# A mixture-of-experts stage in one block, with unscaled rows stored early and two weight places filled before the routing

## What is computed

```python
h = rmsnorm(x, ffn_norm)                              # x * rsqrt(mean(x^2) + eps) * ffn_norm
g_logits = hf @ wg_router + bg_router                 # 4 groups
g_sel = argmax(g_logits); g_w = softmax(g_logits)[g_sel]
e_in = (hf @ we_router + be_router)[:, g_sel]         # 8 experts of that group
top_v, top_i = top_k(e_in, 2)
top_w = softmax(top_v) * g_w
for each of the 32 experts:                           # 1024 -> 256 -> 1024
    hid = silu(hf @ w_gate) * (hf @ w_up) * gates     # gates: top_w of the two chosen experts, else 0
    out += hid @ w_down
x = x + out
```

## Time and profile before

| | us |
|---|---|
| time, median of 3 runs (lowest, highest) | 1571.29 (1565.78, 1571.32) |
| the profiled execution's own time | 1570.89 |
| its span, first to last instruction | 1569.1 |
| PE busy in the span (share) | 1443.5 (92%) |
| DVE busy (share) | 747.6 (48%) |
| ACT busy (share) | 408.3 (26%) |
| POOL busy (share) | 50.4 (3%) |
| bytes moved by DMA | 206.15 MB, mean 131 GB/s |
| granted clock of PE, mean | 0.976 |

### The profile page before, as it was taken

The page is one execution under the profiler, slowest core; times in us unless marked ns, Lnnn a source line. Parts: engine busy times, 40 slices in busy tenths (PEclk is TensorE's granted clock), DMA queues, the critical chain, the costliest instruction groups (busy, mean ns, idle before and its releaser), DMA issues. The chain is left out here.

```text
span 1569.1 us, 13363 instructions
## 1 busy us (share of the span) xinstructions
PE 1443.5 (92%) x4754; PEld 688.1 (44%) x4754; DVE 747.6 (48%) x1657; ACT 408.3 (26%) x645; POOL 50.4 (3%) x120
## 2 busy tenths in 40 slices
PE   7999999999999999999999999998999775998782
PEld 3455555555555544544444344445444433333220
DVE  5567677777676734210134349965333422221113
ACT  2444435444444250000010133133302330000000
POOL 0000000000000000000000000000000001222111
PEclk9999999999999999999999999999999987999996
DMA  7122111221201142222142122010125247999995
GB/s 277 41 97 64 41 49 46 94 65 57 59 22 41 40 175 80 67 70 78 67 160 81 34 80 67 14 58 31 41 73 211 88 195 282 420 427 428 430 410 194
DMA packets 38098, 206.15 MB, mean 131 GB/s; under 512 B 7312, under 2 KB 8336, under 8 KB 30608
## 3 DMA queue, kind: packets, MB, share of 16 engines
q1 hardware_dynamic: 31840, 192.68, 32.8%
q0 software_dynamic: 5040, 8.40, 1.4%
q10 hardware_dynamic: 1152, 4.19, 0.7%
HBM read 202.63 MB, written 12.58 MB: 137 GB/s over the span
## 5 line engine op out<-in xcount | busy, mean ns | idle before, releaser
L442 PE MATMUL gla_proj<-hT,weight_slots 128*128 128x512 f32 x864 | 378.1, 592 | 1.9 <-DVE hT L805 1.9
L442 PEld LDWEIGHTS gla_proj<-hT,weight_slots 128*128 128x128 f32 x864 | 160.9, 190 | 188.8 <-issue 188.1
L907 PE MATMUL bl_p<-hT,weight_slots 128*128 128x512 f32 x256 | 114.3, 600 | 2.1 <-PEq L166 2.1
L2437 PE MATMUL ex_p_gu<-weight_slots,ex_rowsT 128*64 128x512 f32 x432 | 98.6, 604 | 16.7 <-DMA weight_slots<-in_w_gu 14.2
L1268 PE MATMUL mid_p_proj<-hT,weight_slots 128*128 128x512 f32 x208 | 94.7, 604 | 2.3 <-DVE hT L1436 2.3
L907 PEld LDWEIGHTS bl_p<-hT,weight_slots 128*128 128x128 f32 x256 | 48.8, 192 | 62.8 <-issue 62.8
L2573 DVE TENSOR_TENSOR ex_hidden<-ex_silu,ex_p_gu 128x256 f32<-128x256 f32 x16 | 6.7, 421 | 133.9 <-ACT ex_silu L2530 133.9
L596 ACT ACTIVATE gla_level_decay<-gla_level_decay 128x1024 f32<-128x1024 f32 x56 | 59.0, 1057 | 39.3 <-DVE gla_level_decay L725 38.9
L2437 PEld LDWEIGHTS ex_p_gu<-weight_slots,ex_rowsT 128*64 128x64 f32 x432 | 31.6, 138 | 74.9 <-issue 60.0
L1268 PEld LDWEIGHTS mid_p_proj<-hT,weight_slots 128*128 128x128 f32 x208 | 39.7, 193 | 53.8 <-issue 52.7
L943 ACT ACTIVATE bl_sig<-bl_p 128x512 f32<-128x512 f32 x16 | 9.6, 597 | 196.0 <-PE bl_p L907 196.0
(11 more groups left out here) (404 smaller groups left out, 1939.5 us busy)
## 6 DMA issues: line engine op xcount, KB each, us to landing
weight_slots<-in_w_gu SPq DMA_DIRECT2D x27, 2048.0 KB, 29.7
weight_slots<-in_w_dn SPq DMA_DIRECT2D x12, 2048.0 KB, 32.7
weight_slots<-in_w_gla SPq DMA_DIRECT2D x40, 512.0 KB, 3.6
weight_slots<-in_w_merge SPq DMA_DIRECT2D x32, 512.0 KB, 3.9
weight_slots<-in_w_out SPq DMA_DIRECT2D x16, 512.0 KB, 4.5
weight_slots<-in_w_v SPq DMA_DIRECT2D x3, 2048.0 KB, 7.4
xT<-in_w_dn SPq DMA_DIRECT2D x3, 2048.0 KB, 49.3
hT<-in_w_gu SPq DMA_DIRECT2D x3, 2048.0 KB, 19.8
```

The costliest lines, as they stand in the source:

```text
L442: last = nc.tensor.matmul(pj[:, n % 2, :], lhsT, rhs, start=(k == 0), stop=(k == KT - 1))
L907: last = nc.tensor.matmul(pp[:, m % 4, :], core.slot(slot)[:, k, :], src[:, k, :], start=(k == 0), stop=(k == KT - 1))
L2437: last = nc.tensor.matmul(pG[rows, e, :], hgT[:, k, rows], core.as_gate_up(at[k // 4])[:, x, k % 4, :], start=(k == 0), stop=(k == KT - 1))
```

## The change

The three blocks become one. `routing_programs`, `expert_programs` and `combine_programs` return one function for each engine, and `moe_stage` calls them one after the other on each engine, with no barrier between:

```diff
+def moe_stage(core, omT, x_rows, gate, most, ix, ixg, hg, hg_in, out):
+        lot = Lot(core, ctx)
...
+        with nc.Block() as block:
             @block.sync
             def _(sp):
...
+                route[0](sp)
+                experts[0](sp)
+                load_and_store(sp)
```

**SP.** Parts 8 and 9 are issued behind the small loads, ahead of part 4; a place of a first half is free when that half is used; the combination starts when the scatters have landed:

```diff
-                sp.dma_start(iota[:], dram["moe_iota"][:]).then_inc(aux, 16)
+        sp.dma_start(iota, dram["moe_iota"][:, 0:CAP]).then_inc(aux, 16)
+        for c in (8, 9):
+            core.load_part(sp, c)
...
-                sp.wait_ge(h_stored, 16 * NB)
-                core.load_part(sp, 8)
...
-                    core.load_part(sp, PLACES - 1)
...
-                        sp.wait_ge(gu_done if kind == "g" else d_done, u + 1)
+                sp.wait_ge(d_done if kind == "d" else gu_done if h else gu_half, u + 1)
...
+                if k == KT // 2 - 1:
+                    last.then_inc(gu_half, 1)
...
+        first_round()
+        sp.wait_ge(lot.most_ready, 1)
+        with sp.If(sp.value_load(most[0:1, 0:1], min_val=0, max_val=T) > CAP):
...
+        for e in range(2):
+            sp.wait_ge(y_out[e], first_out)
```

**ACT.** The rows are stored as they are turned, without 1 / rms, in three pieces of 512, 256 and 256 columns, and the scaled copies go:

```diff
+        def store(lo, hi):
+            act.dma_start(h_rows[:, :, lo:hi], x_rows[:, :, lo:hi]).then_inc(h_stored, 16)
...
+            if i == 3:
+                store(0, 512)
+            if i == 5:
+                store(512, 768)
+            if i == KT - 1:
+                store(768, D)
...
-                for n in range(NB):
-                    nc.scalar.activation(h_rows[:, n], x_rows[:, n], ACT.Copy, scale=rs[:, n:n + 1]).then_inc(h_scaled, 1)
-                    act.wait_ge(h_scaled, n + 1)
-                    act.dma_start(core.h_rows[n * P:(n + 1) * P, :], h_rows[:, n]).then_inc(h_stored, 16)
```

**1 / rms for the experts.** A second list carries it to the slots: DVE multiplies the one-hot table of the units with `rs`, PE sums it by slot, and each pair's column is copied to `rs2` ahead of the turned rows. It scales gate inside `silu` and up inside `hidden`:

```diff
+        nc.vector.tensor_tensor(four, four, rs.unsqueeze(1).unsqueeze(3).to_broadcast([P, 2, NB, EXPERTS]),
+                                ALU.mult).then_inc(spread_rs, 1)
+        dve.wait_ge(listed, 1)
...
+        dve.wait_ge(listed_rs, 1)
+        chain(nc.vector.tensor_copy(rs_slot[:, 0:PAIRS], pz[:, 0:PAIRS]))
...
+            nc.vector.tensor_copy(rs2[:, e:e + 1], own)
...
+            nc.scalar.activation(sa[:, e], pG[:, e, 0:FF], ACT.Silu, scale=rs2[:, e:e + 1]).then_inc(silu_done, 1)
...
+            nc.vector.scalar_tensor_tensor(out=hid[:, e], in0=pG[:, e, FF:2 * FF], scalar=rs2[:, e:e + 1], in1=sa[:, e],
+                                           op0=ALU.mult, op1=ALU.mult).then_inc(hid_done, 1)
```

**Rounds 2 to 8.** Their lists, with their tables, are now made inside the branch that `most` opens (`list_rounds`), and so are the gathers and turns of the second round's first pairs, which the kernel before issued in any case:

```diff
+        with pe.If(pe.value_load(most[0:1, 0:1], min_val=0, max_val=T) > CAP):
+            list_rounds()
+            turn(PAIRS, 0, 16 * (PAIRS // 2 + 1))
```

More of the change, by code:

```diff
@@ new lines, in scalar, with squares @@
+    def scalar(act):
+        nc.scalar.preload_act_table_set(LN_EXP)
+        def squares(part, lo, hi):
+            if part and lo % 256 == 0:
+                act.wait_ge(sq_out, part)
+            own = lo % 256
+            for n in range(NB):
+                last = nc.scalar.activation(sq[:, n, own:own + hi - lo], x_rows[:, n, lo:hi], ACT.Square,
+                                            accum_out=ss[:, n, part:part + 1])
+            last.then_inc(sq_out, 1)
+        def store(lo, hi):
+            act.dma_start(h_rows[:, :, lo:hi], x_rows[:, :, lo:hi]).then_inc(h_stored, 16)
+        for i in range(KT):
+            act.wait_ge(turned, i + 1)
+            nc.scalar.copy(x_rows[:, :, i * P:(i + 1) * P],
+                           pX[:, i % 2, :].rearrange("p (n c) -> p n c", c=P)).then_inc(rows_out, 1)
+            act.wait_ge(rows_out, i + 1)
+            if i == 3:
+                store(0, 512)
+            if i == 5:
+                store(512, 768)
+            if i == KT - 1:
+                store(768, D)
+            if i % 2 and i < KT - 1:
+                squares(i // 2, (i - 1) * P, (i + 1) * P)
+            if i >= KT - 2:
+                squares(i - 3, i * P, (i + 1) * P)
+        act.wait_ge(ss_ready, 1)
+        nc.scalar.activation(rs, s1, ACT.Ln, bias=core.eps[:, 0:1], scale=1.0 / D).then_inc(rs_ready, 1)
+        act.wait_ge(rs_ready, 1)
+        nc.scalar.activation(rs, rs, ACT.Exp, scale=-0.5).then_inc(rs_ready, 1)
+        act.wait_ge(rs_ready, 2)
+        act.wait_ge(expo, 1)
+        nc.scalar.activation(gx, gx, ACT.Exp).then_inc(expo, 1)
+        act.wait_ge(expo, 3)
+        nc.scalar.activation(m[:, 5], m[:, 5], ACT.Exp).then_inc(expo, 1)
+        nc.scalar.preload_act_table_set(SILU)
@@ L2102, in _ @@
-                project(0)
-                for i in range(1, KT):
-                    project(i)
-                    follow(i - 1)
-                follow(KT - 1)
-                pe.wait_ge(z_out, 1)
-                for n in range(NB):
-                    last = nc.tensor.transpose(ptl[:, n, :], zT[:, n * P:(n + 1) * P], core.ident[0:36, 0:36])
-                last.then_inc(t_done, 1)
-                pe.wait_ge(aux, 80)
-                pe.wait_ge(chosen, 1)
-                nc.tensor.matmul(pR[:, 0:P], before[:], flat(A), start=True, stop=False)
@@ L2124, in _ @@
[L2124 to L2131 removed]
+                route[2](pe)
@@ L2133, in _ @@
+                experts[2](pe)
             @block.scalar
             def _(act):
-                nc.scalar.preload_act_table_set(LN_EXP)
-                def squares(part, lo, hi):
-                    if part:
-                        act.wait_ge(sq_out, 1)
-                    own = (lo - 512) % 512
-                    for n in range(NB):
-                        last = nc.scalar.activation(sq[:, n, own:own + hi - lo], x_rows[:, n, lo:hi], ACT.Square,
-                                                    accum_out=ss[:, n, part:part + 1])
-                    last.then_inc(sq_out, 1)
@@ L2646, in build @@
+                route[4](dve)
+                experts[4](dve)
+                add_up(dve)
 def build(nc, dram, out):
```

1092 lines of the change are left out of this document (577 added, 515 removed).

## The result

The changed kernel takes 1555.36 us (median of 5 runs, 1550.31 to 1557.80) against 1570.55 us (5 runs, 1565.78 to 1571.32): a ratio of 0.9913 with a 95% interval of 0.9887 to 0.9938. The forecast was 1556.0.

A forecast was written before the change was run, and what follows sets the result against it. The prediction took one stream of weight parts to bound the expert stage: part 10 moves by -7.7 + 0.2 - 3.4 = -10.9 us, the end by -4.0 more, so 1570.89 - 14.9 = 1556.0 us, range 1553 to 1559 (8 in 10: 1549 to 1562.5).

The forecast's parts named there:

- The stream: Expert stage: weight parts 10 to 47 saturate DMA until the last down product starts, 211.07 us, unchanged when part 10 moves.
- Item 2: Rows stored unscaled as they turn, so the first gather waits for the list, not the store: -3.7 us.
- The rule cited on the stores: DMA engines serve queues packet by packet, so the last store ends no sooner than the parts: 0 to 1 us.
- item 1: Weight parts 8 and 9 load early, some 1247 us, on idle DMA engines: priced at 0.
- item 3: No block boundary between routing and experts: turning the rows starts 7.7 us sooner, 4.0 of it for the boundary.
- Item 4: List of 1 / rms: one small DVE copy per pair, on the path only for pair 0: +0.2 us.
- Item 5: A place freed in the middle of the first gate/up product lets weight part 10 leave sooner: -3.4 us.
- rival B: TensorE's clock in the first pair: -2.4 us at 2.4 GHz, +2.1 at 1.2 GHz throughout; 12 in 100.
- Item 6: The end: SP waits for the scatters themselves, last down product to combination loads 9.6 us instead of 13.6: -4.0.
- Rival C: Tail gains nothing because engines jump over later rounds' code before the combination: 4.0 us lost, 1560 us; 5 in 100.

The follow-up runs named there:

- the pieces: Changed kernel with weight parts 10 and 11 each loaded in two 1 MB pieces: stage 311.08 us against 311.5 in the changed kernel.
- the order of the products: Changed kernel, parts 10 and 11 in 8 KB-stretch pieces, one expert's four products before the other's, TensorE kept busy: median 1551.87 us, ratio 0.9905 to before.
- the run with late stores: Changed kernel with the rows' three stores issued together when 1 / rms is ready, not as rows turn: stage 317.02 us against 311.5.
- the run with TensorE at work: Changed kernel with 51 useless 128 x 128 products keeping TensorE busy where it waits in the routing: stage 312.11 us against 311.5.

## Why the prediction was right, point by point

- **The stream** (38 parts, 211.07 us) held: 211.15, and 210.93 to 211.15 in the runs that moved only its start. What moves part 10 moves the end, unless TensorE's clock dips at the last but one `down` (212.8 three times) or something in the stream itself changes (the pieces, the order of the products).
- **Item 2, stores, -3.7:** right; the run with late stores gives 4.25 at the gather, 3.74 at part 10. Between the two profiles the gather moved by 4.08, since the list was ready 0.46 sooner behind the router's load (57.47 instead of 57.93), which the item left out. The rule cited on the stores (the Trainium skill, "DMA: Bandwidth & Descriptors", section "Queues, rings and completion order") held here: from 1292 to 1293 SP's queue moved its last 3 packets and ACT's still 109, and the last 0.5 MB, issued at 1277.27, took 16.3 us to land. Of the 8 us of lead that the item leaned on, 0.9 were left to the list at 1294.43. In the run with TensorE at work the list was 1.2 us earlier and ran into the store.
- **Items 1 and 3, the failed attribution:** turn 0 was forecast at -7.7 and came at -7.74, with the path as told: the gather lands, PE turns. But item 1 priced the early fills at 0 and item 3 booked their gain as "-4.0 for the boundary". Undone alone, the fills cost 5.2 us and the boundary 0.4 at the turn and 0.0 in the stage: the boundary waited for the gather, and the gather for the part ahead of it. Between the two profiles 3.7 us were won from the gather's start to the turn; 7.0 of the 8.1 before were flight and 1.1 the boundary behind it, and 4.4 in all are left, so some 2.6 are the fills' and 1.1 the boundary's. 5.0 of the 5.85 us of DVE's idle time in the earlier trace rows were that flight, not the boundary's price.
- **Item 4, +0.2:** turn to `gate_up` went from 3.37 to 3.53.
- **Item 5, -3.4:** the half is worth that: part 10 left 3.43 us ahead of the end of `gate_up` 0 (1309.30 against 1312.73), and the run without it gives 3.13 at part 10, with a `gate_up` 0 that was 0.34 shorter. From `gate_up`'s start to part 10 only 2.75 were won, since the clock was 0.50 until well into `gate_up` 0, and it took 9.34 us instead of 8.65: its half 5.93, not 5.2. The sum took its length as fixed. That is rival B's lower side.
- **Item 6, -4.0:** 4.8 by the profiles; the landing took 3.5 us, not 4.1. What was saved is not mainly a boundary (1.4) but GpSimd's reading and branching behind the landing (2.9), which now lie beside the scatter. Rival C feared the branches as a new cost of the merged block; they had been a cost in the kernel before.
- **The sum:** -14.9 against -15.26 in the stage. That it is so close is in part luck: 0.7 too much in item 5 and 0.8 too little in item 6 cancel. The profiled execution itself came 5.7 us below 1556.0, 5.3 of it ahead of the stage, a spread that the range had from the runs only in part; the median met it.

## What to carry to other kernels

Before pricing a barrier from the idle time in front of it, find what is in flight there: here it waited for a DMA that waited for a weight part, and moving the part freed more (some 2.6 us) than removing the barrier (1.1). Name the chain that ends at the head of a saturated stream and price each change by that head alone. Compare profiles from the first instruction of the changed stage on, since the code ahead of it can differ by more than the effect sought.

## What the runs showed of the hardware that was not expected

- TensorE's granted clock can fall to 0.50 for 3.4 us while it is at work. From 1299.7 to 1303.1 in one run PE was busy throughout. In three runs the fall met the last but one `down` and cost 1.7 us; in the one shown it lay from 1521.2 to 1524.6 and began 0.3 us after a stretch of 2.0 us in which PE had waited for weights. The same wait was 1.85 us long in most of the runs without the fall. The profiles differ by up to 6.3 us at the stage's start.
- A gather of 128 rows landed in 4.4 us on idle engines, in 7.0 behind one part of 2 MB issued ahead of it, and in 10.5 behind two.
- Pieces of 1 MB in stretches of 4 KB ran at 304 and 338 GB/s, in stretches of 8 KB at 379 to 389, whole parts at 409 to 413, with the engines 0.93 to 0.98 busy each time.
- Products with 64 columns of weights and 512 columns of rows are 0.44 us each (7.09 / 16) when they alternate between the two halves of the output's partitions, 0.56 on average (8.94 / 16) when four in a row go to one half.
